# One float32 product for the scatter of expert rows, in place of three bfloat16 parts

## The reference: one decoder step with a mixture of experts

```
logits = t @ router_w + router_b          # t: 320 x 1024, 32 experts
vals, idx = top_k(logits, 4); gates = softmax(vals)
y = 0
for e in range(32):
    a = min(t @ w_gate[e] + b_gate[e], 7)
    u = clip(t @ w_up[e] + b_up[e], -7, 7)
    hid = (u + 1) * a * sigmoid(1.702 * a)
    y = y + combine[:, e:e+1] * (hid @ w_down[e] + b_down[e])
```

## Time and profile before

| | |
|---|---|
| Time, median of 3 runs | 1152.35 us (1152.32 to 1152.73) |
| The profiled execution | 1152.4 us, its span in the trace 1150.5 us |
| Busy | PE 1108.7 us (96%), DVE 400.1 (35%), ACT 161.8 (14%), POOL 23.7 (2%) |
| Granted clock of PE | 0.997 in the mean |
| Read from HBM | 428.26 MB, 375 GB/s over the span |

### The profile page before, as it was taken

The page is one execution under the profiler, slowest core; times in us unless marked ns, Lnnn a source line. Parts: engine busy times, 40 slices in busy tenths (PEclk is TensorE's granted clock), DMA queues, the critical chain, the costliest instruction groups (busy, mean ns, idle before and its releaser), DMA issues.

```text
span 1150.5 us, 15105 instructions
## 1 busy us (share of the span) xinstructions
PE 1108.7 (96%) x6045; PEld 464.8 (40%) x6045; DVE 400.1 (35%) x711; ACT 161.8 (14%) x283; POOL 23.7 (2%) x51
## 2 busy tenths in 40 slices
PE   8999999999999999999999999999999999999996
PEld 5786764433333333333333333333333333333332
DVE  4155185633333333333333332222233333333333
ACT  3100114311111111111111111111111111111112
POOL 0002000000000000000000000000000000000000
PEclk9999999999999999999999999999999999999998
DMA  9970308599999999999999999999999999999992
GB/s 314 332 219 1 147 28 331 228 405 430 414 426 434 434 432 431 432 432 431 433 433 428 433 434 427 434 433 428 433 434 428 433 434 430 431 435 432 430 426 101
DMA packets 35389, 432.30 MB, mean 376 GB/s; under 512 B 2527, under 2 KB 17699, under 8 KB 21797
## 3 DMA queue, kind: packets, MB, share of 16 engines
q1 hardware_dynamic: 33712, 428.13, 89.0%
q0 software_dynamic: 848, 3.03, 0.7%
q10 hardware_dynamic: 805, 0.82, 0.2%
HBM read 428.26 MB, written 3.71 MB: 375 GB/s over the span
## 4 chain that ended last, share of the span: by engine, by line
PE 75%; DMA 21%; ACT 2%; DVE 2%; issue 0%; SPq 0%; ACTq 0%; DVEq 0%
PE ps L1339 44%; DMA ring<-in_w_gate 21%; PE ps L1073 9%; PE ps L1316 5%; PE ps L1190 3%; PE ps L1238 3%; PE ps L1325 2%; PE ps L1382 2%; PE ps L1241 2%; ACT R L577 1%; PE ps L1063 1%; PE ps L1100 1%; PE ps L1298 1%; DMA consts<-in_consts 0%; PE ps L1208 0%
## 5 line engine op out<-in xcount | busy, mean ns | idle before, releaser
L1339 PE MATMUL ps<-ring,R 128*64 128x512 f32 x3072 | 690.0, 595 | 13.2 <-DMA ring<-in_w_gate 13.2
L1339 PEld LDWEIGHTS ps<-ring,R 128*64 128x64 f32 x3072 | 209.8, 136 | 410.8 <-issue 382.1
L930 DVE SCALAR_TENSOR_TENSOR x<-ps,gates,x 128x1024 f32<-128x1024 f32 (+1 forms) x96 | 106.2, 1106 | 133.7 <-PE ps L1316 133.7
L1073 PE MATMUL ps<-R,ring 128*128 128x320 f32 x384 | 107.4, 436 | 0.6 <-DVE R L657 0.6
L936 DVE TENSOR_TENSOR R<-ps,R 128x512 f32<-128x512 f32 x32 | 22.1, 692 | 240.4 <-ACT R L580 240.4
L969 DVE TENSOR_SCALAR R<-ps 128x512 f32<-128x512 f32 x32 | 22.1, 692 | 187.9 <-PE ps L1339 187.9
L1073 PEld LDWEIGHTS ps<-R,ring 128*128 128x128 f32 x384 | 71.7, 190 | 31.1 <-issue 1.8
L1316 PE MATMUL ps<-R 64*128 64x512 bf16 (+1 forms) x576 | 79.3, 381 | 0.0
L573 ACT ACTIVATE R<-R 128x512 f32<-128x512 f32 x32 | 20.2, 632 | 307.4 <-DVE R L967 307.4
L1316 PEld LDWEIGHTS ps<-R 64*128 64x128 bf16 (+1 forms) x576 | 21.4, 98 | 88.8 <-issue 51.9
L557 ACT ACTIVATE R<-ps 128x512 f32<-128x512 f32 x33 | 19.7, 598 | 234.3 <-PE ps L1241 234.3
(11 more groups left out here) (220 smaller groups left out, 601.3 us busy)
## 6 DMA issues: line engine op xcount, KB each, us to landing
ring<-in_w_gate SPq DMA_DIRECT2D x30, 4096.0 KB, 28.4
ring<-in_w_up SPq DMA_DIRECT2D x28, 4096.0 KB, 29.3
ring<-in_w_down SPq DMA_DIRECT2D x28, 4096.0 KB, 31.1
ring<-in_w_up SPq DMA_DIRECT2D x8, 2048.0 KB, 11.7
ring<-in_w_down SPq DMA_DIRECT2D x8, 2048.0 KB, 12.7
ring<-in_w_in SPq DMA_DIRECT2D x14, 1024.0 KB, 12.6
ring<-in_w_gate SPq DMA_DIRECT2D x4, 2048.0 KB, 9.7
ring<-in_w_out SPq DMA_DIRECT2D x4, 1024.0 KB, 8.9
```

The source lines that it names most:

```text
L930: STT(xb[b], rows, gates[:, par, b:b + 1], xb[b], ALU.mult, ALU.add).then_inc(accDone, 1)
L1073: ins = MM(ps[:, n % 2, 0:NT], slot_k(L, 256)[:, k, 128 * half:128 * half + 128], hT[:, k, :], start=(k == 0), stop=(k == KT - 1))
L1339: ins = MM(shape(ps[64 * half:64 * half + 64, bank, :]), lhs(k), cols(w, half), start=False, stop=(k == KT - 1))
```

## The change

The rows are kept in float32, `ysb` is one tile of 128 x 512 that ACT copies from PSUM, and PT is float32. The scatter is one product for each block and half. The two roundings and two subtractions and their semaphores go. The core of the diff:

```diff
-        ysb = R1[:, 4608:5120].bitcast(bf16).rearrange("p (s d) -> p s d", s=2)
-        ysb = [ysb[:, 0, :], ysb[:, 1, :], R4[:, 2240:2496].bitcast(bf16)]
+        ysb = view(R1, 4608, shape=(512,))
...
-        PT = R4[:, 1920:1920 + NT].bitcast(bf16).rearrange("p (n t) -> p n t", n=2)
+        PT = view(R4, 1920, "p (n t) -> p n t", shape=(2, NT), n=2)
...
                         act.wait_ge(scatMM, e * 3 + 3 + START)
-                        act.activation(ysb[0], ps[:, 2, :], ACT.Copy).then_inc(yHigh, 1)
-                        act.wait_ge(yRest, e + 1 + START)
-                        act.activation(ysb[1], yrest, ACT.Copy).then_inc(yMid, 1)
+                        act.activation(ysb, ps[:, 2, :], ACT.Copy).then_inc(yOutS, 1)
...
-                def split_rows(e):
-                    dve.wait_ge(yHigh, e + 1 + START)
-                    dve.wait_ge(yMid, e + START)
-                    TT(yrest, ps[:, 2, :], ysb[0], ALU.subtract).then_inc(yRest, 1)
-                    dve.wait_ge(yMid, e + 1 + START)
-                    dve.wait_ge(yRest, e + 1 + START)
-                    TT(ysb[2], yrest, ysb[1], ALU.subtract).then_inc(yLow, 1)
...
-                    for part in range(3):
-                        for half in range(2):
-                            to = ps[:, 6 + half, :] if b < 2 else ps[64 * half:64 * half + 64, 6, :]
-                            ins = MM(to, PT[64 * half:64 * half + 64, par, t0:t0 + n],
-                                     ysb[part][64 * half:64 * half + 64, :], start=(part == 0), stop=(part == 2))
+                    for half in range(2):
+                        to = ps[:, 6 + half, :] if b < 2 else ps[64 * half:64 * half + 64, 6, :]
+                        ins = MM(to, PT[64 * half:64 * half + 64, par, t0:t0 + n], ysb[64 * half:64 * half + 64, :],
+                                 start=True, stop=True)
                     ins.then_inc(scatMM, 1)
...
-            for part, ready in enumerate((yHigh, yMid, yLow)):
-                pe.wait_ge(ready, E + START)
-                for b, (t0, n) in enumerate(TOK):
+            pe.wait_ge(yOutS, E + START)
+            for b, (t0, n) in enumerate(TOK):
```

More of the change, by code:

```diff
@@ L124, in hybrid_shortconv_hgrn2_moe_step @@
         x2T = view(R3, 3072, "p (k t) -> p k t", shape=(8, 128), k=8)
-        ga, gs, gu, gt, xgs, xgT, hidT, yrest, hid = [view(R3, 512 * n, shape=(512,)) for n in range(9)]
-        ysb = R1[:, 4608:5120].bitcast(bf16).rearrange("p (s d) -> p s d", s=2)
-        ysb = [ysb[:, 0, :], ysb[:, 1, :], R4[:, 2240:2496].bitcast(bf16)]
+        ga, gs, gu, gt, xgs, xgT, hidT, _, hid = [view(R3, 512 * n, shape=(512,)) for n in range(9)]
+        ysb = view(R1, 4608, shape=(512,))
         cv = view(R4, 0, "p (c t) -> p c t", shape=(4, NT), c=4)
@@ L210, in hybrid_shortconv_hgrn2_moe_step @@
         lastMM = sem("last_mm")
-        yHigh, yRest, yMid, yLow = sem("y_high"), sem("y_rest"), sem("y_mid"), sem("y_low")
+        yOutS = sem("y_copied")
         aloneP, aloneV, aloneT = sem("alone_pool"), sem("alone_dve"), sem("alone_pe")
@@ L424, in _ @@
         def _(act):
-            credit(act, sigDone, xgOut, gtOut, hidTOut, yHigh, yMid)
+            credit(act, sigDone, xgOut, gtOut, hidTOut, yOutS)
             act.dma_start(parRows[:], A["par_rows"]).then_inc(parIn, 16)
@@ L614, in need @@
                     dve.wait_ge(s, n)
-            credit(dve, posShift, prep, gatesDone, yRest, yLow, aDone, uDone, tDone, hidDone, xgTOut, accDone)
+            credit(dve, posShift, prep, gatesDone, aDone, uDone, tDone, hidDone, xgTOut, accDone)
             TT, TS, STT = dve.tensor_tensor, dve.tensor_scalar, dve.scalar_tensor_tensor
@@ L947, in one_round @@
                     dve.memset(gates[:, 1, :], 0.0)
-                    dve.memset(ysb[0], 0.0)
-                    dve.memset(ysb[1], 0.0)
-                    dve.memset(ysb[2], 0.0).then_inc(zeroed, 1)
+                    dve.memset(ysb, 0.0).then_inc(zeroed, 1)
                     dve.wait_ge(zeroed, 1)
@@ L979, in one_round @@
                         gathered(m)
-                        split_rows(e)
                 dve.wait_ge(prep, p0 + (E + 1) + START)
@@ L1365, in scatter_before @@
                             if b == 0:
-                                pe.wait_ge(yLow, e + START)
-                                pe.wait_ge(yMid, e + START)
+                                pe.wait_ge(yOutS, e + START)
                                 pe.wait_ge(gtOut, m0 + START)
@@ L1385, in one_round @@
                         pe.wait_ge(hidTOut, e + 1 + START)
-                        pe.wait_ge(yRest, e + START)
+                        pe.wait_ge(yOutS, e + START)
                         product(2, 2, half_c(hidT), e, it, j)
@@ L1390, in close_round @@
                 p0, e0 = r * (E + 1), r * E
-                pe.wait_ge(yMid, e0 + E + START)
-                pe.wait_ge(yLow, e0 + E + START)
+                pe.wait_ge(yOutS, e0 + E + START)
                 pe.wait_ge(accDone, (e0 + E) * 3 + START)
@@ L1404, in _ @@
             pe.wait_ge(gtOut, (E + 1) + START)
-            for part, ready in enumerate((yHigh, yMid, yLow)):
-                pe.wait_ge(ready, E + START)
-                for b, (t0, n) in enumerate(TOK):
[L1408 to L1413, removed]
+            pe.wait_ge(yOutS, E + START)
+            for b, (t0, n) in enumerate(TOK):
+                for half in range(2):
+                    to = ps[:, LAST[b] + half, :] if b < 2 else ps[64 * half:64 * half + 64, LAST[b], :]
+                    ins = MM(to, PT[64 * half:64 * half + 64, 1, t0:t0 + n], ysb[64 * half:64 * half + 64, :], start=True, stop=True)
+                ins.then_inc(lastMM, 1)
             pe.wait_ge(finSq, 3)
```

## The result

| | before | changed |
|---|---|---|
| Median | 1152.34 us (1151.25 to 1152.73) | 1164.49 us (1162.93 to 1167.23) |
| Ratio | | 1.0104, 95% interval 1.0090 to 1.0118 |
| The profiled execution | 1152.4 us, span 1150.5 | 1165.6 us, span 1163.8 |

The account below looks back on a forecast made before the run. Loads at 432 GB/s were taken to bound the loop once TensorE's lead is used up, leaving 16.5 us of waits. +27.2 on TensorE, -16.5 of waits, -1.4 behind the loop: +9.3, 1161.7 us (1156.5 to 1168).

Parts of the forecast that it names:

- What bounds the kernel: Expert loop: TensorE uses up its lead, then goes at the loads' pace; 16.5 us is waiting, 0.52 us an expert.
- The price of a float32 scatter: TensorE in the expert loop: 1.05, 1.05 and 1.01 us for the three blocks, 0.85 us an expert more.
- the sum of under 3 us: End result if the first float32 weight load hid as well as the bfloat16 one, near 0.65 us an expert.
- A load laid bare before the second pass: Rival, scatters: second pass's weights don't load under the first; 0.5 us an expert more, 1177.7 us; chance 0.05.
- Halves one after the other: Rival, scatters: 0.86 us more for each block, 2.6 an expert, +92, 1244 us; chance 0.03.
- Swallowed by the waits: Rival, loop: waits for weights take all of it, below 0.52 us an expert; 1151 to 1154 us; within 0.2% 0.07.
- The room at the addition: Rival: the 0.38 us before scatters 2 and 3 goes; 3 to 20 us more, 1165 to 1182; chance 0.08.
- The work taken from ACT and DVE: Loop: one ACT copy of 0.6 us and two DVE subtractions of 0.69 us an expert go, gaining nothing.
- The loads after the change: Loop: TensorE at 28.90 us an expert doesn't wait for loads; 924.8 us against 914.2, +10.7 us.
- the bound of 3.4 us: Early experts: most the loads can lose to later ring slot releases, 0.85 us an expert over four experts.
- Behind the loop: After the last expert: with one part the first addition starts at about 1138.8 instead of 1140.21, -1.4 us.
- The sum: Whole kernel: +27.2 on TensorE, -16.5 of waits, -1.4 at the end, +9.3 us, median 1161.7 us.

Follow-up runs that it names:

- half loads: From the fifth matrix on, each load brings half of its bytes: the kernel before took 1135.89 us, the changed kernel 1163.62 us.
- a dose of 0.43 us an expert: Kernel before with one more bfloat16 pass in the scatters of the first two blocks: 1154.26 us against 1151.58, ratio 1.0021.
- one of 1.29: Kernel before with two more bfloat16 passes in each of the three scatters: 1178.26 us, ratio 1.0226.
- the kernel with two parts: Kernel before without its third bfloat16 part (its subtraction and its passes): 1150.77 us against 1152.37, ratio 0.9997.

## Why the prediction was right

- **What bounds the kernel.** Right. The 16.5 us of waits were measured as 16.5 with half loads. Of a dose of 0.43 us an expert, 13.8 in all, 0.8 us stood in the loop of the trace and 2.7 in the median; one of 1.29 cost what exceeds the reserve (+25.0 us in the loop of its trace, 24.8 worked out).
- **The price of a float32 scatter.** 1.05, 1.05, 1.01 us were forecast and 1.06, 1.06, 1.00 came: 0.855 us an expert in place of 0.85. The row that carried it was the earlier trace rows, a product of another shape in which separate array rows work at once. The weight loads took 184 and 131 ns. By the formula of the Trainium skill (TensorE: Matmul & The Clock Gate, "LDWEIGHTS (loading the stationary operand)") they would take 107 and 53; this trace doesn't agree, and the sum of under 3 us worked out from it didn't come.
- **The rivals.** A load laid bare before the second pass: no, the whole scatter has no room for it. Halves one after the other: not in the loop, where half the matmuls take the same time; the third block behind the loop is another matter, see below. Swallowed by the waits: no, 0.855 is above 0.52; the dose of 0.43 shows that below this nearly all of it goes into the waits. The room at the addition: unchanged at 0.38 us. The rule of the Trainium skill (TensorE: Matmul & The Clock Gate, "The mechanism") that loads overlap only for another row group doesn't agree with this trace, where the second pass's weights loaded on the same rows within the first 0.30 us of a scatter of 1.06. The same section also lets a load into a background weight buffer be pulled ahead; no trace here shows which buffer a load goes to.
- **The work taken from ACT and DVE.** Worth nothing in the loop, as forecast.
- **The loads after the change.** TensorE doesn't wait. Counted from the start of the loop, expert 31's gate matrix lands 1.7 us later than before (887.9 in place of 886.2), inside the bound of 3.4 us.
- **Behind the loop.** -1.2 us in place of -1.4. The first addition came as forecast, but the step that has the third block's products done before DVE comes to them was wrong: its halves start 0.77 us apart, and the three additions take 3.31 us in place of 3.13. In the seven traces with this float32 scatter behind the loop the second half is late by 0.5 to 1.1 us in six and starts together with the first in one (that with half of each scatter left out in the loop). The profile names only "issue"; the cause is open.
- **The sum.** +9.3 forecast. The loop gave +10.8 (10.7), the end -1.2. In a pair of traces without either loss ahead of the loop (the kernel before, and the changed one measured again) the spans differ by 10.0, 0.45 of it ahead of the loop. The medians differ by 12.2, 11.2 and 11.5 in the three pairs, 2 to 3 us beyond the forecast. In the first pair of profiles the excess is in the part before the loop, which the sum had put at nothing. For the medians this is inferred, since only the profiled executions show where their time went. What was left out is that this part varies in both kernels, and that one profile can't show it. The range held the result partly because it had been made wide for other reasons.

## What to carry to other kernels

Where a stream of loads and an engine share the bound, work out the reserve in us from the starts of the rounds, and compare each edit's price with the reserve for a round: here 0.43 us an expert cost 0.8 us of its 13.8 in the trace's loop (2.7 in the median), and 0.855 cost 10.8 of its 27.4. Three bfloat16 passes took less of TensorE here than one float32 product, and the split that they need lay beside other work: two float32 instructions last as long as four bfloat16 passes (0.43 us a piece against 0.215, by the doses), and the second float32 pass came 0.1 us later still, behind the first weights. A profile of one execution says nothing of how a part varies: take the part's length from several traces before a term is put at zero.

## What the runs showed of the hardware that was not expected

- TensorE's clock in the first 20 us varies from run to run of one and the same program. In the changed kernel it was 0.72 or 1.00 from 14 to 20 us, which is worth 1.7 us. And the half pace of the start ended by 6.6 us in one trace and after 11.4 and 11.7 in two, worth 1.4 to 1.6 us; the clock column shows 1.00 there.
- Behind the loop the two float32 halves of the third block started 0.5 to 1.1 us apart in six of seven traces, while the same pair starts together in the loop.
- In the kernel with two parts, PE and DVE both stood still for about 1.1 us behind the loop, with "issue" as the only name in the trace.
